# Two extra 512-wide matmuls per item in the last two attentions of a two-model block

## The chip, the cores and the metric

The kernel runs on one core of a Trainium2 chip. The metric is the time of one execution on the device in microseconds (us), as the median of several runs. The clock of TensorE (PE in the rows) is granted by a throttle at one of two levels; a row shows it as a share, where 1.00 is 2.4 GHz and 0.50 is 1.2 GHz.

## What is computed

Two small transformer stacks run one after the other over 256 tokens of width 1024, in fp32 accuracy. The first has a convolution and pooling mixer, a sparse latent attention with a gated recurrence ("dsa" in the kernel), two cross attentions ("x0", "x1") and two expert layers over all 16384 experts. The second, with which the change deals, has two layers:

```python
h = h + even_mixer(rmsnorm(h))   # layer 0: latent causal attention (8 heads) and dilated attention (8 heads)
h = h + swiglu(rmsnorm(h))
h = h + odd_mixer(rmsnorm(h))    # layer 1: sliding window attention with sinks, 16 query heads, 2 kv heads
h = h + swiglu(rmsnorm(h))
```

Each head of these attentions is softmax(q k^T * scale + bias) v, causal over 256 keys. A latent head has 96 dimensions for q and k and 64 for v; all others have 64 and 64. The outputs of all 16 heads go through a 1024 x 1024 projection (e_out, then o_out).

## The kernel before

All engines run one program each, written out by hand, and meet at semaphores. Weights come as a stream of blocks of 128 x 1024; ACT splits each into a high part wH (L483) and DVE or POOL into a low part wL (L493), and both lie in four buffers. A linear layer does three one-pass matmuls for each product (L699 high by high, L700 low by high, L701 high by low), so that the sum is as good as fp32. The attentions use plain fp32 operands instead, which take several passes.

TensorE's results go to 8 banks of PSUM in a fixed order of "groups". bank(key) takes the next group, and reused(n) waits until the group that held the same bank before has been read. w(key) waits on w_low for the block's low part.

attention(kind, ...) runs all attentions. An item is a head and a query tile tt of 128 tokens; with tt = 0 it sees 128 keys, with tt = 1 it sees 256. "mla" (layer 0: heads 0 to 7 latent, 8 to 15 dilated) and "swa" (layer 1) have 16 heads, so 32 items, and the loop has 32 + 5 = 37 turns. In turn i TensorE does the scores S of item i (L756), the transposes PT of the probabilities of item i - 2 (L765), and the product O with the values of item i - 5 (L774). DVE adds the bias (L1542), takes the maximum (L1553) and scales the output (L1559, L1561); ACT takes the exponential (L1184) and copies the transposed probabilities back (L1193). After the loop 16 transposes (L783) turn the outputs, ACT and DVE split them (L1133, L1498), and the projection begins. At the start of the loop TensorE does S of items 0, 1 and 2 and then waits for the probabilities of item 0.

The score matmuls have the head's dimensions as their rows: 96 in the latent heads, 64 in the others. Before an attention all weight blocks that fit into the four buffers are split; in the attention no block is consumed.

Of the kernel before, what the change touches and what calls it, by code (L numbers as in the profile page):

```python
# [18 lines left out]
P = 128  # L19
# [7 lines left out]
NBUF = 4  # L27
# [46 lines left out]
def attention_items(kind):  # L74

    heads = {"x0": 4, "x1": 4, "dsa": 8, "mla": 16, "swa": 16}[kind]
    return [(h, tt) for h in range(heads) for tt in range(NT)]
# [3 lines left out]
DEEP = 4  # L81
AHEAD = 40
POOLED = AHEAD + 3


CKV, IK, IQ, HQ, HF, HG = 8, 9, range(10, 14), range(14, 18), range(18, 22), range(22, 26)
# [197 lines left out]
def build_stacks(nc, x, mem, vecs, cst, w_stream, iw_w, sinks, rel_bias, c_cnt, c_neg, c_masks, c_bucket,  # L284
# [15 lines left out]
    bank_of, before, holder, turn = [], [], {}, 0  # L300
# [9 lines left out]
    with ExitStack() as ctx:  # L310
        def sb(name, shape, dt=F32):
            return ctx.enter_context(nc.sbuf_tensor(name, shape, dt))

        def sem(name):
            return ctx.enter_context(nc.semaphore(name))

        def stage(*wanted):

            with ExitStack() as scope:
                held = [scope.enter_context(nc.sbuf_tensor(name, [P] + list(shape), dt)) for name, shape, dt in wanted]  # L320
                return [t[tuple([slice(None)] * (len(w[1]) + 1))] for t, w in zip(held, wanted)]
# [8 lines left out]
        _, memH, memL = stage(("mem_before", [MEM0], F32), ("memH", [DC, T], F32R), ("memL", [DC, T], F32R))  # L330
        _, att_L, att_P, att_PT, att_O, att_OTH, att_OTL = stage(
            ("att_before", [ATT0], F32), ("att_L", [DEEP, 258], F32), ("att_P", [DEEP, 258], F32),
            ("att_PT", [DEEP, 256], F32), ("att_O", [2, 1024], F32), ("att_OTH", [8, 256], F32R),
            ("att_OTL", [8, 256], F32R))
# [9 lines left out]
        _, rel_bucket, rel_rows = stage(("rel_before", [MEM0 - 1024], F32), ("rel_bucket", [512], F32),  # L344
                                        ("rel_rows", [512], F32))
# [47 lines left out]
        wH, wL = sb("wH", [P, NBUF, BLK], F32R), sb("wL", [P, NBUF, BLK], F32R)  # L393
# [11 lines left out]
        psum = [ctx.enter_context(nc.psum_tensor(f"bank{i}", [P, 512], F32)) for i in range(ALL_BANKS)]  # L405
# [27 lines left out]
        w_high, w_low = sem("w_high"), sem("w_low")  # L433
# [51 lines left out]

        pools = [range(BNO[(f"peer{l}q", 8, 0)], BNO[(f"peer{l}u", 0)] + POOLED) for l in range(2)]

        def split_low(eng, b, i=0):

            if isinstance(i, int) and any(b in (r.start, r.stop) for r in pools):  # L490
                eng.wait_ge(w_low, b)
            eng.wait_ge(w_high, i * 4 + (b + 1))
            eng.tensor_tensor(wL[:, b % NBUF, :], raw(b), wH[:, b % NBUF, :].bitcast(F32),  # L493
                              ALU.subtract).then_inc(w_low, 1)
# [6 lines left out]
        def feed(eng, n):  # L501

            if id(eng) not in fed:
                return
            nxt, split, own = fed[id(eng)]
            while nxt < len(blocks) and (nxt < NBUF or last_read(nxt - NBUF) < n):
                if own(nxt):
                    split(eng, nxt)
                nxt += 1
            fed[id(eng)][0] = nxt  # L510

        def read_of(eng, key):

            n = NO[key]
            feed(eng, n)
            eng.wait_ge(read_by[reader[n]], rank[n])
# [13 lines left out]
        def att_span(kind, tt):  # L530

            return T if kind in ("x0", "x1") else (tt + 1) * P
# [17 lines left out]
        def probs_done(eng, kind, j):  # L550

            if kind in ("x0", "x1"):
                read_of(eng, (kind, "S", j))
            else:
                feed(eng, NO[(kind, "S", j)])
                eng.wait_ge(att_probs, probs_base[kind] + j + 1)
# [114 lines left out]
        def _(pe):  # L671
            at = [0]
            stands = [0]

            def bank(key):

                n = NO[key]
                assert n == at[0], (key, n, at[0])
                at[0] += 1
                reused(n)  # L680
                return psum[bank_of[n]]

            def reused(n):

                if before[n] is not None:
                    pe.wait_ge(read_by[reader[before[n]]], rank[before[n]])
# [47 lines left out]
            def token_major(keys, wkeys, src, cols=512, first=0):  # L734

                for tt, key in enumerate(keys, first):
# [5 lines left out]
                                       k == 0, k == DC - 1)  # L742
                    last.then_inc(group_done, 1)

            def attention(kind, q_of, k_of, v_of):
                items = attention_items(kind)
                base = att_base[kind]
                hv = ATT_V[kind]
                for i in range(len(items) + ATT_LAG_O):
                    if i < len(items):  # L750
                        hd, tt = items[i]
                        span = att_span(kind, tt)
                        ps = bank((kind, "S", i))
                        qs, ks = q_of(hd), k_of(hd)
                        for c in range(len(qs)):
                            last = pe.matmul(ps[:, 0:span], qs[c][:, tt * P:(tt + 1) * P], ks[c][:, 0:span],  # L756
                                             start=(c == 0), stop=(c == len(qs) - 1))
                        last.then_inc(group_done, 1)
                    j = i - ATT_LAG_PT
                    if 0 <= j < len(items):  # L760
                        hd, tt = items[j]
                        ps = bank((kind, "PT", j))
                        probs_done(pe, kind, j)
                        for s in range(att_span(kind, tt) // P):
                            last = pe.transpose(ps[:, s * P:(s + 1) * P], att_P[:, j % DEEP, s * P:(s + 1) * P], ident)  # L765
                        last.then_inc(group_done, 1)
                    j = i - ATT_LAG_O
                    if 0 <= j < len(items):
                        hd, tt = items[j]
                        ps = bank((kind, "O", j))  # L770
                        read_of(pe, (kind, "PT", j))
                        ns = att_span(kind, tt) // P
                        for s in range(ns):
                            last = pe.matmul(ps[:, 0:hv], att_PT[:, j % DEEP, s * P:(s + 1) * P], v_of(hd, s),  # L774
                                             start=(s == 0), stop=(s == ns - 1))
                        last.then_inc(group_done, 1)
                read_of(pe, (kind, "O", len(items) - 1))
                for tt in range(NT):
                    for half in range(2):
                        ps = bank((kind, "OT", tt, half))  # L780
                        for c in range(4):
                            cc = half * 4 + c
                            last = pe.transpose(ps[:, c * P:(c + 1) * P], att_O[:, tt, cc * P:(cc + 1) * P], ident)  # L783
                        last.then_inc(group_done, 1)
# [197 lines left out]
            for tt in range(NT):  # L982
                ps = bank(("iw", tt))
                for k in range(DC):
                    for part in hn:
                        last = pe.matmul(ps[:, 0:8], part[:, k, tt * P:(tt + 1) * P].bitcast(F32), iww[:, k, :],
                                         start=(k == 0 and part is hn[0]), stop=(k == DC - 1 and part is hn[1]))
# [14 lines left out]
            for hd in range(4):  # L1002
                last = pe.matmul(ps[:, hd * P:(hd + 1) * P], kl[:, hd * P:(hd + 1) * P], ql[:, hd * P:(hd + 1) * P],
                                 start=True, stop=True)
# [9 lines left out]
            for hd in range(4):  # L1014
# [5 lines left out]
                          stop=True).then_inc(group_done, 1)  # L1020
# [447 lines left out]
        def _(dve):  # L1468
# [100 lines left out]
            def peer(l):  # L1569
# [67 lines left out]
                def rows(i, j):  # L1637
                    if not isinstance(i, int) or j >= 2:

                        dve.wait_ge(g_done, i * 4 + (l * T // 4 + j - 1))  # L1640
                    for m in range(4):
                        k = (4 * j + m) % 8
                        tok = i * 16 + (4 * j + m)
                        dve.tensor_scalar(onehot[:, k, :], iota, slotT[:, 2, bass.ds(tok, 1)], None, ALU.is_equal)  # L1644
                        last = dve.tensor_scalar(onehot[:, 8 + k, :], iota, slotT[:, 1, bass.ds(tok, 1)],  # L1645
                                                 slotT[:, 0, bass.ds(tok, 1)], ALU.is_equal, ALU.mult)
                    last.then_inc(onehots, 1)
# [13 lines left out]
                for j in range(4):  # L1661
                    rows(0, j)
                    split_low(dve, b0 + POOLED + j)
                with dve.Fori(1, T // 16) as i:
                    for j in range(4):
                        rows(i, j)
                        split_low(dve, b0 + POOLED + j, i)
                with dve.Fori(0, (N_KEYS - AHEAD - T // 4) // 4) as i:
                    for j in range(4):
                        split_low(dve, b0 + POOLED + T // 4 + j, i)  # L1670
                dve.wait_ge(g_read, (l + 1) * T // 4)
# [457 lines left out]
```

## Time and profile before

| | us |
|---|---|
| median of 3 runs | 3132.38 |
| lowest, highest | 3124.88, 3133.9 |
| profiled execution | 3136.3 |
| its span | 3134.5 |
| PE busy | 2918.3 (93%) |
| DVE busy | 1978.9 (63%) |
| ACT busy | 1466.4 (47%) |
| mean granted clock of PE | 0.94 |

By line, the chain that ended last is PE at L699 22%, L700 21%, L701 21%, then the splits of weights (POOL 4%, DVE 3%, ACT 3%) and, of the attentions, L756 2% and L774 2%, L765 1%. The profile is one execution. PE's busy time counts an instruction from its start to its modelled end; neighbouring matmuls overlap, so distances between starts tell their pace better than their durations. The granted clock is a record of its own and is shown for any stretch of time.

### The profile page before, as it was taken

To read this page: it belongs to the slowest core of one execution; us is meant where nothing else is said; L and a number is where in the kernel's file an instruction comes from. 1 tells how busy PE (TensorE), PEld (TensorE's weight loads), DVE (VectorE), ACT (ScalarE), POOL (GpSimd) and SP (SyncE) were. 2 spreads that over 40 slices of the span, in tenths; PEclk is the share of its full clock that TensorE was granted. 3 is DMA by queue.
4 is the path that set the end of the run, shared out by engine and by line. 5 is a ranking of instruction groups with operands and counts; after the bars stand their busy time and mean duration, and the time that the engine had idled before them with its cause. 6 is when DMAs were issued, how large, how long until landed. Compare 5 with 4: busy or idle time off the path is not lost.

```text
span 3134.5 us, 57237 instructions
## 1 busy us (share of the span) xinstructions
PE 2918.3 (93%) x19610; PEld 2711.0 (86%) x19610; DVE 1978.9 (63%) x4205; ACT 1466.4 (47%) x2397; POOL 338.8 (11%) x167
## 2 busy tenths in 40 slices
PE   7889799999999998968999999999997899999998
PEld 6889699999988887858998999988886779987998
DVE  6545942886577676685597887466775655445554
ACT  5444344444455555444444444455554444443443
POOL 0003685000000000000277000000000000000000
PEclk9998899999999999889899999999998879995999
DMA  4434366445666663322456445676664315450444
GB/s 155 153 148 148 134 211 199 172 171 188 230 250 239 241 242 132 121 78 98 149 178 210 174 170 186 217 254 238 245 236 149 120 54 177 176 220 6 162 182 155
DMA packets 140448, 546.16 MB, mean 174 GB/s; under 512 B 15784, under 2 KB 81592, under 8 KB 83616
## 3 DMA queue, kind: packets, MB, share of 16 engines
q1 hardware_dynamic: 63216, 455.38, 40.1%
q10 hardware_dynamic: 73728, 67.14, 6.9%
q0 software_dynamic: 3376, 21.88, 1.8%
q8 instruction: 86, 1.41, 0.2%
q14 instruction: 42, 0.34, 0.0%
HBM read 505.53 MB, written 40.91 MB: 174 GB/s over the span
## 4 chain that ended last, share of the span: by engine, by line
PE 74%; DVE 9%; DMA 6%; ACT 5%; POOL 4%; issue 2%; SPq 0%; ACTq 0%; DVEq 0%
PE bank L699 22%; PE bank L700 21%; PE bank L701 21%; POOL wL L493 4%; PE bank L855 4%; ACT wH L483 3%; DVE wL L493 3%; DMA ring<-in_w_stream 3%; DMA act_parked<-act_out 2%; PE bank L756 2%; PE bank L774 2%; PE bank L765 1%; PE bank L712 1%; DVE act_out L1486 1%; DVE h L1518 1%
## 5 line engine op out<-in xcount | busy, mean ns | idle before, releaser
L493 DVE TENSOR_TENSOR wL<-ring,wH 128x1024 fp32r<-128x1024 f32 x744 | 906.9, 1225 | 750.9 <-ACT wH L483 750.3
L699 PE MATMUL bank<-hnH,wH 128*128 128x256 f32 x3648 | 1066.9, 292 | 61.2 <-DVE hnL L1492 44.1
L700 PE MATMUL bank<-hnL,wH 128*128 128x256 f32 x3648 | 1045.4, 287 | 0.0
L701 PE MATMUL bank<-hnH,wL 128*128 128x256 f32 x3648 | 1044.7, 286 | 0.0
L483 ACT ACTIVATE wH<-ring 128x1024 fp32r<-128x1024 f32 x864 | 906.3, 1055 | 274.0 <-DMA ring<-in_w_stream 128.6
L699 PEld LDWEIGHTS bank<-hnH,wH 128*128 128x128 f32 x3648 | 711.6, 195 | 71.8 <-issue 57.7
L700 PEld LDWEIGHTS bank<-hnL,wH 128*128 128x128 f32 x3648 | 714.5, 196 | 0.1
L701 PEld LDWEIGHTS bank<-hnH,wL 128*128 128x128 f32 x3648 | 712.8, 195 | 0.0
L699 PE MATMUL bank<-wH,wgtH 128*128 128x512 f32 x1024 | 400.1, 391 | 4.5 <-issue 4.5
L700 PE MATMUL bank<-wL,wgtH 128*128 128x512 f32 x1024 | 399.5, 390 | 0.0
L701 PE MATMUL bank<-wH,wgtL 128*128 128x512 f32 x1024 | 399.5, 390 | 0.0
L493 POOL TENSOR_TENSOR wL<-ring,wH 128x1024 fp32r<-128x1024 f32 x120 | 314.6, 2641 | 140.6 <-ACT wH L483 140.5
L1244 ACT ACTIVATE act_out<-bank 128x256 f32<-128x256 f32 x256 | 98.1, 383 | 393.5 <-PE bank L701 334.7
L699 PEld LDWEIGHTS bank<-wH,wgtH 128*128 128x128 f32 x1024 | 192.9, 188 | 45.0 <-issue 5.1
L1268 ACT ACTIVATE wgtH<-gates 128x256 fp32r (+1 forms) x256 | 107.2, 419 | 258.0 <-PE bank L701 257.7
L701 PEld LDWEIGHTS bank<-wH,wgtL 128*128 128x128 f32 x1024 | 193.0, 188 | 40.4
L700 PEld LDWEIGHTS bank<-wL,wgtH 128*128 128x128 f32 x1024 | 193.1, 189 | 40.2
L1645 DVE TENSOR_SCALAR onehot<-con,slotT 128x128 f32<-128x128 f32 x512 | 175.2, 342 | 0.0
L1644 DVE TENSOR_SCALAR onehot<-con,slotT 128x128 f32<-128x128 f32 x512 | 144.1, 281 | 18.6 <-ACT slotT L1283 18.6
L855 PE MATMUL bank<-onehot 128*128 128x128 f32 x1024 | 136.3, 276 | 8.8 <-DVE onehot L1645 8.8
L855 PEld LDWEIGHTS bank<-onehot 128*128 128x128 f32 x1024 | 126.5, 193 | 9.2 <-DVE onehot L1645 9.2
L1152 ACT ACTIVATE sq<-h 128x256 f32<-128x256 f32 x96 | 37.0, 415 | 181.1 <-DVE h L1518 172.0
(338 smaller groups left out, 3612.7 us busy)
## 6 DMA issues: line engine op xcount, KB each, us to landing
ring<-in_w_stream SPq DMA_DIRECT2D x432, 1024.0 KB, 4.9
act_parked<-act_out ACTq DMA_DIRECT2D x256, 128.0 KB, 3.6
act_in<-act_parked ACTq DMA_DIRECT2D x256, 128.0 KB, 2.7
sw_bias<-in_c_swa POOLq DMA_DIRECT2D x1, 4096.0 KB, 13.9
relb_rows<-rel_table POOLq DMA_DIRECT2D x1, 2048.0 KB, 9.6
h_parked<-h POOLq DMA_DIRECT2D x2, 1024.0 KB, 6.5
h_back<-h_parked POOLq DMA_DIRECT2D x2, 1024.0 KB, 6.3
od_relb<-relb_rows POOLq DMA_DIRECT2D x2, 1024.0 KB, 8.2
```

What stands on the lines that cost most here:

```text
L483: eng.activation(wH[:, b % NBUF, :], raw(b), ACT.Copy).then_inc(w_high, 1)
L493: eng.tensor_tensor(wL[:, b % NBUF, :], raw(b), wH[:, b % NBUF, :].bitcast(F32), ALU.subtract).then_inc(w_low, 1)
L699: pe.matmul(dst, lh, rh, start=start, stop=False, skip_group_check=True)
L700: pe.matmul(dst, lh, rl, start=False, stop=False, skip_group_check=True)
L701: return pe.matmul(dst, ll, rh, start=False, stop=stop, skip_group_check=True)
L756: last = pe.matmul(ps[:, 0:span], qs[c][:, tt * P:(tt + 1) * P], ks[c][:, 0:span], start=(c == 0), stop=(c == len(qs) - 1))
L774: last = pe.matmul(ps[:, 0:hv], att_PT[:, j % DEEP, s * P:(s + 1) * P], v_of(hd, s), start=(s == 0), stop=(s == ns - 1))
L855: last = pe.matmul(psacc[j][:, m * P:(m + 1) * P], onehot[:, k, :], onehot[:, 8 + k, :], start=True, stop=True)
L1244: act.activation(act_out[:, c % 2, :], psum[c % BANKS][:, 0:T], ACT.Gelu_apprx_tanh).then_inc(u_read, 1)
L1268: act.activation(wgtH[:, c % 2, :].unsqueeze(1), gates[:, bass.ds(i * 4 + c, 1), :], ACT.Copy).then_inc(wgt_high, 1)
L1644: dve.tensor_scalar(onehot[:, k, :], iota, slotT[:, 2, bass.ds(tok, 1)], None, ALU.is_equal)
L1645: last = dve.tensor_scalar(onehot[:, 8 + k, :], iota, slotT[:, 1, bass.ds(tok, 1)], slotT[:, 0, bass.ds(tok, 1)], ALU.is_equal, ALU.mult)
```

## The change

A function spin() is added for TensorE. It runs behind the O product of a turn, in the attentions mla and swa alone, from turn 2 on. It looks up the next group's bank, waits until that bank may be written, waits for the next weight block that is not used yet, and runs SPINS = 2 matmuls with that block's high part as both operands (128 columns of it as the stationary one, 512 as the moving one). The result lands in the next group's bank, whose own first matmul overwrites it (start=True). No semaphore is raised.

```diff
+SPINS = 2
...
+            def spin():
+
+                b, n = stands[0], at[0]
+                reused(n)
+                pe.wait_ge(w_low, b + 1)
+                for _ in range(SPINS):
+                    pe.matmul(psum[bank_of[n]][:, :], wH[:, b % NBUF, 0:P], wH[:, b % NBUF, 0:512], start=True, stop=True)
+
             def attention(kind, q_of, k_of, v_of):
...
                         last.then_inc(group_done, 1)
+                    if kind in ("mla", "swa") and i >= 2:
+                        spin()
                 read_of(pe, (kind, "O", len(items) - 1))
```

## Rows read from the trace of the kernel before

**Rows 1.** The page: granted clock of PE in 40 slices, in tenths.
```profile
PEclk9998899999999999889899999999998879995999
```

**Rows 2.** Table by stretch: start:end, us, busy per engine (instructions), PEclk, DMA share, GB/s.
```profile
core 0: us, PE busy (x) PEld busy (x) DVE busy (x) ACT busy (x) POOL busy (x), PEclk, DMA share, GB/s
...
2490.00:2507.00 17.00, 17.00 (x70) 15.22 (x70) 11.25 (x43) 8.14 (x32) 0.00 (x0) 0.50 0.01 1
2508.00:2536.00 28.00, 28.00 (x93) 20.20 (x93) 14.93 (x57) 10.93 (x45) 0.00 (x0) 0.50 0.00 1
...
2542.00:2546.40 4.40, 3.68 (x16) 3.28 (x16) 2.15 (x4) 2.12 (x4) 0.00 (x0) 0.50 0.00 0
2546.40:2550.00 3.60, 2.48 (x21) 2.49 (x22) 0.90 (x2) 0.27 (x1) 0.00 (x0) 1.00 0.00 0
2827.00:2879.00 52.00, 52.00 (x171) 37.36 (x170) 29.64 (x132) 20.74 (x82) 0.00 (x0) 0.50 0.00 1
...
2890.80:2894.60 3.80, 3.76 (x17) 3.76 (x18) 0.00 (x0) 0.00 (x0) 0.00 (x0) 0.50 0.01 4
```

**Rows 3.** Chain that ended last in mla: start, us, engine and line.
```profile
2508.11 1.15 PE bank L756 x2
...
2535.87 1.15 PE bank L756 x2
```

**Rows 4.** The same chain in swa: one pair, and the last pair's start.
```profile
2831.50 1.15 PE bank L756 x2
2832.65 0.62 PE bank L765 x2
2833.27 0.32 PE bank L774 x2
2833.59 0.72 PE bank L756 x2
2834.32 0.40 PE bank L765
2834.72 0.75 PE bank L774 x4
...
2879.13 1.15 PE bank L756 x2
```

**Rows 5.** Table by stretch around TensorE's gap, mla and swa.
```profile
2484.98:2488.40 3.42, 1.43 (x9) 1.09 (x10) 3.14 (x9) 2.35 (x8) 0.00 (x0) 1.00 0.73 287
...
2819.50:2822.90 3.40, 2.04 (x15) 1.65 (x13) 1.21 (x2) 2.45 (x3) 0.00 (x0) 1.00 0.70 280
```

**Rows 6.** Table by stretch in the dsa attention.
```profile
1368.00:1372.00 4.00, 4.00 (x17) 3.35 (x17) 3.64 (x13) 2.37 (x9) 0.00 (x0) 0.50 0.01 4
...
1376.00:1384.00 8.00, 5.63 (x35) 4.19 (x36) 7.43 (x27) 3.94 (x16) 0.00 (x0) 1.00 0.00 0
```

**Rows 7.** Timeline of two 512-wide matmuls at the low clock.
```profile
2480.88 0.63 PE L699 MATMUL bank<-wH,ml_nH 128*128 128x512 f32 x1
...
2481.31 0.52 PE L700 MATMUL bank<-wL,ml_nH 128*128 128x512 f32 x1
```

**Rows 8.** Table by stretch in the outs loop of an expert layer.
```profile
900.00:1100.00 200.00, 200.00 (x884) 165.62 (x883) 140.17 (x221) 108.55 (x147) 0.00 (x0) 1.00 0.68 242
```

**Rows 9.** Chain that ended last: the last weight split before swa.
```profile
2821.69 1.23 DVE wL L493
```

**Rows 10.** Timeline: output transposes and the product behind them, dsa and mla.
```profile
1389.32 1.97 PE L783 MATMUL bank<-con,att_O 128*128 128x128 f32 x16 [0.77 <-DVE att_O L1561]
...
1393.60 0.39 PE L699 MATMUL bank<-att_OTH,wH 128*128 128x256 f32 x1 [2.32 <-DVE att_OTL L1498]
...
2542.36 3.68 PE L783 MATMUL bank<-con,att_O 128*128 128x128 f32 x16 [0.45 <-DVE att_O L1561]
...
2547.52 0.39 PE L699 MATMUL bank<-att_OTH,wH 128*128 128x256 f32 x1 [1.48 <-DVE att_OTL L1498]
```

## The prediction

> **What bounds the kernel now.** I read the page's clock line first [rows 1]: it is 9 over most of the span, with 7 in the 33rd slice and 5 in the 37th. The question is what lies in those two and what TensorE does there. The table by stretch answers it [rows 2]. In the first half of the "mla" attention (heads of 96 rows) TensorE is busy 17.00 of 17.00 us at a granted clock of 0.50, in its second half (64 rows) 28.00 of 28.00 at 0.50, in "swa" 52.00 of 52.00 at 0.50. 0.50 is the lower level, 1.2 GHz. DVE is busy 14.93 of 28 and 29.64 of 52 us, ACT less. So both attentions are bound by TensorE's own stream at half clock, over 97 us of these three rows alone, and no wait sets their pace.
>
> The chain of waits shows it at a finer grain. Two items (one head, both query tiles) are a repeating pair. In the 64-row heads the big score product starts at 2508.11 and for the seventh time after it at 2535.87 [rows 3], so a pair takes 27.76 / 7 = 3.97 us. In swa [rows 4] it is again 3.97: 1.15 + 0.62 + 0.32 + 0.72 + 0.40 + 0.75 = 3.96, with no piece of another engine, and 2831.50 to 2879.13 are 12 pairs. A 96-row pair is 13 matmul records, and 70 of them stand in 17.00 us: 3.2 us.
>
> Why the clock is down: before each attention TensorE runs dry until the first softmax is out. Around that gap it was busy 1.43 of 3.42 us (mla) and 2.04 of 3.40 (swa), still at 1.00 [rows 5], and right behind these stretches the clock is 0.50, to the end of the attention. The "dsa" attention tells what can bring it back [rows 6]: after its gap it too ran at 0.50, busy 4.00 of 4.00 us to 1372 with matmuls of all 128 rows, and by 1376 the clock had risen; it stayed at 1.00 though TensorE was then busy only 5.63 of 8.00. So a full-height stream raised it; the mix of 96 or 64 rows with 64-column outputs did not, in 28 and 52 us without a pause; and a far thinner mix keeps it once it is up.
>
> **The change part by part.** It removes and moves nothing. It adds, from i = 2 to 36 of the 37 turns of each of the two loops, two matmuls: 35 x 2 = 70 per attention, 140 in all, 128 rows by 512 columns in the one-pass type.
>
> *Price of one.* At the low clock the nearest rows are two 512-wide products of the va group, whose starts lie 2481.31 - 2480.88 = 0.43 us apart [rows 7]; 70 are 30.1 us. At the full clock the outs loop of the expert stage has 884 of them in 200.00 us, 0.226 each [rows 8]; 70 are 15.8 us. Their weight loads are inside both numbers.
>
> *The waits it adds.* reused(n) waits for the reader of the bank which the next group would wait for anyway. w_low waits for the first block of the output projection; it is split in order, and the last split before swa starts at 2821.69 [rows 9], before the first turn that spins, and none is made in the attention. I take 0 for both; if a reader were late, everything queued on TensorE would stand behind it, but the next group would have stood there too. No DMA is added, and SP, POOL, ACT and DVE get no instruction.
>
> *mla, if the clock comes back.* At full clock a 96-row pair's own work is 3.2 / 2 = 1.6 us, with four added matmuls 1.6 + 0.9 = 2.5: a gain of 0.7. A 64-row pair is 3.97 / 2 + 0.90 = 2.89: a gain of 1.08. DVE needs about 14.93 / 28 x 3.97 = 2.1 us for a pair, so it is not yet the bound. From 2488.4, where the clock fell, to 2508.1 are 6.2 pairs of the first kind: -4.3 us. Then 7 of the second: -7.6. The last turns, 6.5 us from 2535.87 to the transposes at 2542.36, become 3.25 + 6 x 0.45 = 5.95: -0.5. The transposes of the output: in dsa at 1.00 from their start to the next product 1393.60 - 1389.32 = 4.28 us, in mla at 0.50 it is 2547.52 - 2542.36 = 5.16 [rows 10]: -0.9. Two turns that ran at 1.00 before 2488.4 get 0.9 dearer. Sum -12.4. I take off 2.9 for hand-overs at the tighter pace (about 0.1 a pair, 1.3) and for one turn or two of a first stretch at low clock (1.6), and say -9.5, with -13 to -5 as its range.
>
> Will it come back here? The mix with the added work lies between the 96-row mix that stayed at 0.50 and the 128-row mix that rose. About a third of its time (1.7 of 4.9 us in a pair at low clock) is now the full-height stream, and the rest is three quarters high. That is near to dsa's, so I say yes, and soon. The 64-row half then inherits the full clock, and dsa shows that keeping it takes little.
>
> *swa, if the clock stays down.* It has no 96-row half: it starts cold, since the first added matmul comes behind the first transpose, that is behind the same gap. Its own pair is 3.97 us with half-height score products, the added 1.7 us of full height make 30% of 5.7 us. That is further from dsa's mix than mla's is, and its neighbour in the trace is the 64-row mix at 0.50. I take low clock to the end: 70 x 0.43 = 30.1 us, all on the path, since the chain is TensorE throughout. A weight load that the long matmul now hides can give back some: a 64-row big product takes 1.15 in the chain, and 0.2 of that over 16 pairs is 3 us. Bounds 25 to 31, taken 29.
>
> *Sum.* -9.5 + 29 = +19.5 us. The profiled execution took 3136.3 us (span 3134.5); that gives 3155.8. The median of the runs shown is 3132.4, 3.9 lower; on it the forecast is 3152.
>
> **What the Trainium skill says to this.** The row first: from 2542.00 to 2546.40 TensorE ran 16 transposes and nothing else, at 0.50, and behind them the clock is 1.00 [rows 2]. "TensorE: Matmul & The Clock Gate", Part 4, says that work in transpose mode does not count as activity for the clock in the same way. By that rule the transposes in the loop would weaken the mix, and the third rival below would gain; the trace disagrees, and I keep that rival small. The same page, Part 1, has it that activity releases the throttle; taken as busy time it would give these stretches the full clock already, and the added matmuls would cost 140 x 0.226 = 32 us and buy nothing. The rows at 28.00 of 28.00 and 0.50 speak against that reading.
>
> **The rivals.**
> (a) *Both attentions come back to the full clock* (the other side). Mechanism: the full-height share is enough for the 64-row mix too, or swa's clock doesn't fall at all because the added matmuls fill waits behind the gap. For it: dsa rose within a few us of such a stretch; swa offers over 52 us in which a denser moment could do. Against: 52.00 us at 0.50 without the clock ever rising. Price: 12 pairs in [rows 4] and 2 before them, 14 x -1.08 = -15.1; one pair at the low clock first +2.8; last turns -0.5; transposes -0.9; the output projection, which now spends its first 3.8 us at 0.50 [rows 2], -1.9; hand-overs +1.4: -14.2. With mla's -9.5 that is -23.7: 3109 us. The point from which it decides: each cold swa pair costs 4 x 0.43 = 1.72, each warm one gives 1.08; with mla's 9.5 and the 3 of the ends the whole comes out at zero if the clock rises at about the tenth of 14 pairs, and faster if earlier.
> (b) *Neither comes back* (the added matmuls are load and nothing else). For it: both stages sat at 0.50 though TensorE was never idle. Against: dsa. Price: 29 in each, +58: 3190 us.
> (c) *swa rises late*, somewhere past the middle, or mla late: within 9 us of before, or in between.
>
> **How the numbers follow.** Forecast 0.56; (a) 0.28; (b) 0.07; (c) 0.09, of which 0.06 lies within 0.3%, 0.02 faster, 0.01 slower. The bound of 0.3%, 9.4 us, is about what a measurement of this kernel can tell from no change. So faster 0.30, same 0.06, slower 0.64. The forecast's own range is its parts' bounds, 25 - 13 to 31 - 5: +12 to +26, or 3144 to 3158, and some more for the scatter of the medians (3124.9 to 3133.9 before): to 3163. As (a) holds 0.28, the range for 8 in 10 goes down to it: 3104 to 3163.
>
> **What would show it.** The clock by stretch: 1.00 in mla from a few us behind its first transposes on, 0.50 in swa. Pairs of 2.5 to 2.6 us and 2.9 to 3.0 in mla, 5.5 to 5.7 in swa. The added matmuls 0.23 apart in mla, 0.43 in swa. The clock rising only after the start of the output projection behind swa. The forecast is wrong if swa's row shows 1.00 (then the mix of row heights was no bar), or if mla's shows 0.50; and its sizes are wrong if DVE's share goes to 0.9 at full clock, as then the added matmuls are hidden under DVE.

## The result, and the profile after

The changed kernel takes 3149.12 us (median of 7 runs, 3143.15 to 3160.76) against 3133.9 (7 runs, 3124.88 to 3139.85): ratio 1.0053, 95% interval 1.0034 to 1.0073. The medians lie 15 us apart, and the ratio makes it some 17. The forecast was 3152 on a median of 3132.4. The profiled execution took 3143.15 us, its span is 3141.4.

The table by stretch of the kernel after (start:end, us, busy time by engine, granted clock, DMA) answers to [rows 2] and [rows 5]. The first five rows are mla, the last three swa.

```profile
core 0: us, PE busy (x) PEld busy (x) DVE busy (x) ACT busy (x) POOL busy (x), PEclk, DMA share, GB/s
2471.80:2475.20 3.40, 1.99 (x6) 1.55 (x7) 1.94 (x7) 1.92 (x8) 0.00 (x0) 0.50 0.71 289
2475.20:2478.60 3.40, 3.40 (x12) 2.92 (x11) 1.42 (x4) 1.52 (x6) 0.00 (x0) 0.50 0.00 0
2478.60:2492.00 13.40, 13.40 (x90) 11.92 (x90) 10.25 (x41) 7.63 (x30) 0.00 (x0) 1.00 0.01 2
2493.00:2518.00 25.00, 25.00 (x132) 15.96 (x131) 16.08 (x62) 12.05 (x48) 0.00 (x0) 1.00 0.00 1
2523.40:2527.20 3.80, 1.87 (x16) 1.63 (x16) 2.48 (x4) 2.06 (x4) 0.00 (x0) 1.00 0.00 0
...
2810.00:2886.00 76.00, 76.00 (x221) 48.23 (x221) 29.12 (x130) 20.15 (x81) 0.00 (x0) 0.50 0.00 1
2886.00:2891.60 5.60, 5.60 (x18) 3.70 (x18) 1.88 (x9) 1.26 (x5) 0.00 (x0) 0.50 0.00 0
2891.60:2895.20 3.60, 3.60 (x24) 2.98 (x23) 1.35 (x7) 0.38 (x1) 0.00 (x0) 0.99 0.02 7
```

TensorE is busy all the time in both, as before. What differs is the clock: in mla it is 0.50 for 6.8 us from the gap on and then 1.00 to the end, where it was 0.50 from 2488.4 on to the end of the attention; in swa it is 0.50 for the 76 and 5.6 us of two rows, and comes back in the last turns only, where no score products are left.

The stages can be measured from the first score product to the first product of the projection. The timeline of the kernel before has for the start of mla and the end of TensorE's idle time behind it (2.21 us), and for the start and end of swa (the end of mla is in [rows 10]):

```profile
2483.46 1.14 PE L756 MATMUL bank<-ml_k,ml_q 96*128 96x128 f32 x6 [0.71 <-ACT ml_vA L1160]
...
2486.81 0.30 PE L765 MATMUL bank<-con,att_P 128*128 128x128 f32 x1 [2.21 <-ACT att_P L1184]
...
2820.77 1.14 PE L756 MATMUL bank<-sw_k,sw_q 64*128 64x128 f32 x6 [0.37 <-ACT sw_v L1160]
...
2890.84 0.58 PE L699 MATMUL bank<-att_OTH,wH 128*128 128x256 f32 x1 [1.48 <-DVE att_OTL L1498]
```

and the kernel after, mla and swa:

```profile
2469.75 1.14 PE L765 MATMUL bank<-ml_k,ml_q 96*128 96x128 f32 x6 [0.99 <-ACT ml_vA L1171]
...
2527.24 0.39 PE L700 MATMUL bank<-att_OTH,wH 128*128 128x256 f32 x1 [1.97 <-DVE att_OTL L1509]
...
2800.85 1.14 PE L765 MATMUL bank<-sw_k,sw_q 64*128 64x128 f32 x6 [0.36 <-ACT sw_v L1171]
...
2899.02 0.39 PE L700 MATMUL bank<-att_OTH,wH 128*128 128x256 f32 x1 [1.97 <-DVE att_OTL L1509]
```

(The lines have moved: scores L765, transposes L774, outputs L783, output transposes L794, the added matmuls L752.) mla: 64.06 us before, 57.49 after, -6.6. swa: 70.07 before, 98.17 after, +28.1. Together +21.5. The spans differ by 6.9 only, because this execution reached mla 13.7 us earlier, through code that was not changed. The experiments below show that as scatter: with the front part always the same, mla begins between 2474 and 2485 us in them, while a stage repeats within 0.1 us as long as the clock moves at the same places. So stages are compared below, and medians beside them.

One such place differs in mla itself. In the kernel before the clock fell at about 2488.3, which is 4.9 us after the first score product; in the kernel after it fell at 2471.8, 2.1 us after it. An unchanged mla in which it also fell 2.1 us after the start took 64.78 us (the run with the matmuls in swa alone, below). Against that one the change gives mla -7.3 us; 0.7 of it is missing from the -6.6 because the kernel before had the full clock a little longer.

The chain of waits after (start, us, engine and line) has one pair of items in the 64-row half of mla, then one in swa, and around it the big score products of swa's items 5 and 31:

```profile
2494.33 0.62 PE bank L765 x2
2494.95 0.37 PE bank L774 x2
2495.32 0.17 PE bank L783 x2
2495.49 0.52 PE bank L752 x2
2496.01 0.41 PE bank L765 x2
2496.43 0.26 PE bank L774
2496.69 0.39 PE bank L783 x4
2497.08 0.52 PE bank L752 x2
...
2810.20 1.15 PE bank L765 x2
...
2827.88 1.15 PE bank L765 x2
2829.03 0.62 PE bank L774 x2
2829.65 0.32 PE bank L783 x2
2829.97 0.96 PE bank L752 x2
2830.93 0.72 PE bank L765 x2
2831.65 0.41 PE bank L774
2832.05 0.75 PE bank L783 x4
2832.81 0.96 PE bank L752 x2
...
2886.75 1.15 PE bank L765 x2
```

The own work of the swa pair is 3.97 us, the same pieces as in [rows 4]; two pairs of added matmuls of 0.96 make it 5.89. In mla the same kind of pair takes 3.26 us (the sum of its pieces; 3.27 by the starts): own work 2.22, added 1.04.

### The profile page after: what moved, and what is told of

Its sections match the earlier page's. It is cut to its first block, busy times and chain, and to the rows that moved or that the text cites. A ratio compares the mean times of both kernels' runs of the same rounds, so it can differ in the third digit from the quotient of the medians.

```text
span 3141.4 us, 57587 instructions
## 1 busy us (share of the span) xinstructions
PE 2921.8 (93%) x19750; PEld 2699.1 (86%) x19750; DVE 1976.4 (63%) x4205; ACT 1464.1 (47%) x2397; POOL 338.6 (11%) x167
## 4 chain that ended last, share of the span: by engine, by line
PE 73%; DVE 9%; DMA 6%; ACT 5%; POOL 4%; issue 2%; SPq 0%; ACTq 0%; DVEq 0%
PE bank L700 21%; PE bank L702 20%; PE bank L701 20%; POOL wL L494 4%; DMA ring<-in_w_stream 4%; PE bank L866 4%; ACT wH L484 3%; DVE wL L494 3%; DMA act_parked<-act_out 2%; PE bank L752 2%; PE bank L765 2%; PE bank L783 1%; PE bank L774 1%; PE bank L713 1%; DVE act_out L1497 1%
```

## Experiments

**One attention at a time.** Which of the two carries which sign.

```diff
-                    if kind in ("mla", "swa") and i >= 2:
+                    if kind == "mla" and i >= 2:
```

> The added matmuls stand in mla alone, swa is as before. My theory (the full-height work brings the clock back in mla, not in swa): the mla stage, from its first score product to the first product of the projection, is about 57.5 us as in the changed kernel (64.1 before), clock 1.00 in it but for its first 7 us or so; swa 70 us as before. Time 6.6 us under the kernel before, 3127, ratio 0.998. Rival (the two attentions work on each other, or the scatter of the rest of the kernel hides it): mla over 62 us, ratio 1.000 or more.

Measured: 3125.94 us, ratio 0.9977 (0.9966 to 0.9988), 7 us under before. mla 57.52 us, swa 70.08. Both are the stages expected, each to 0.1 us: what is added in mla does not act on swa.

```diff
-                    if kind in ("mla", "swa") and i >= 2:
+                    if kind == "swa" and i >= 2:
```

> The added matmuls stand in swa alone. My theory: clock 0.50 in swa to the end of the loop, pairs of 5.9 us, the swa stage 98 us against 70 before, time +28 us, 3162, ratio 1.009; mla 64 us at 0.50. Rival (swa's clock stayed down by accident of that one execution): the clock is 1.00 in most of swa, the stage is under 70 us and the time at or under the kernel before.

Measured: 3154.63 us (4 runs), ratio 1.0076 (1.0051 to 1.0102), 7 us less than expected. swa 98.18 us with some 88.7 of them at 0.50, mla 64.78. That swa stays at the low clock is no accident of one execution. The table by stretch of both versions, each in its mla and then its swa; the first two rows are the version with the matmuls in mla alone:

```profile
2491.40:2539.80 48.40, 46.46 (x273) 34.49 (x271) 32.65 (x122) 23.35 (x87) 0.00 (x0) 1.00 0.00 1
2822.00:2883.00 61.00, 59.51 (x205) 44.40 (x205) 34.09 (x147) 23.69 (x87) 0.00 (x0) 0.50 0.00 1
...
2480.20:2538.00 57.80, 57.31 (x212) 45.91 (x210) 32.94 (x124) 24.45 (x93) 0.00 (x0) 0.50 0.00 1
2815.00:2903.00 88.00, 86.98 (x250) 54.85 (x251) 34.15 (x152) 24.26 (x95) 0.00 (x0) 0.50 0.00 1
```

**Half the rows.** The forecast rested on the height of the rows: mla's 96 against swa's 64. This tests it inside mla, by the added matmuls themselves. They write one bank further on; a control writes that same bank with 128 rows.

```diff
-                b, n = stands[0], at[0]
+                b, n = stands[0], at[0] + 1
...
-                    pe.matmul(psum[bank_of[n]][:, :], wH[:, b % NBUF, 0:P], wH[:, b % NBUF, 0:512], start=True, stop=True)
+                    pe.matmul(psum[bank_of[n]][:, :], wH[0:64, b % NBUF, 0:P], wH[0:64, b % NBUF, 0:512], start=True, stop=True)
...
-                    if kind in ("mla", "swa") and i >= 2:
+                    if kind == "mla" and i >= 2:
```

> As mla alone, but the added matmuls use 64 rows of the tile instead of 128 and write the bank after the next one. Same count, same columns, same busy time. If the height of the rows counts for the clock: it stays 0.50 in mla, the stage is 64 + 70 x 0.48 = about 97 us. If busy time or columns alone count: it rises as with 128 rows, stage about 57 us.

> The control for the version with 64 rows: mla alone, two matmuls of 128 rows and 512 columns per turn, written to the bank after the next one. If rows were what counted: as with the next bank, mla stage about 57.5 us, clock 1.00 but for its first us. If the other bank was what kept the clock down: 0.50 and about 98 us as with 64 rows.

Measured with 64 rows: 3173.17 us (2 runs), ratio 1.013 (1.0096 to 1.0164), mla 98.32 us. With 128 rows: 3128.16, ratio 0.9986 (0.9967 to 1.0004), mla 57.52. The table by stretch has the whole of mla with 64 rows in its first row, then mla with 128 rows from the rise of the clock on:

```profile
2483.10:2579.40 96.30, 93.31 (x288) 63.68 (x288) 36.87 (x133) 27.30 (x101) 0.00 (x0) 0.50 0.03 10
...
2490.50:2539.00 48.50, 46.56 (x273) 34.59 (x271) 32.68 (x122) 23.43 (x87) 0.00 (x0) 1.00 0.00 1
```

Same count, same columns, TensorE busy 93.31 of 96.30 us, and the clock never comes back. Halving the rows turned a gain of 7 us into a loss of 34 in the stage. So being busy, with the same matmuls and columns per turn, did not raise the clock here; what made the difference was the height of the added matmuls, by itself or by what it brings with it.

It brings a second change with it, in the pace. The chain of waits has the same first turns in the kernel after (two rows) and with 64 rows (the next two), from the first added pair to the fourth score product; the last two rows are two pairs of items further on, with 64 rows:

```profile
2473.65 0.87 PE bank L752 x2
...
2478.15 0.74 PE bank L765 x2
...
2485.07 1.15 PE bank L752 x2
...
2491.03 1.15 PE bank L765 x2
...
2526.21 0.85 PE bank L765 x2
...
2536.29 0.85 PE bank L765 x2
```

Both at 0.50, the same work took 4.50 us with 128 rows and 5.96 with 64, so it came a quarter less densely. In the 64-row half of mla it came faster: 10.08 us for two pairs is 5.04 a pair, less than the 5.89 of swa. Whether the height alone held the clock down, or partly the slower pace, is not separated.

**Four instead of two in swa.**

```diff
-                        spin()
+                        spin(SPINS if kind == "mla" else 2 * SPINS)
```

> Two added matmuls per turn in mla, four in swa. If swa stayed cold because the full-height share of its mix was too small, four bring the clock to 1.00: a pair is then 1.99 + 8 x 0.26 = 4.1 us, the swa stage about 72 to 76 us, less than with two (98), time about 3132 + 4 - 7 = 3130. If something else holds the clock down in swa, a pair is 3.97 + 8 x 0.48 = 7.8 us, the stage about 130 us, time about 3185.

Measured: 3138.15 us (10 runs, 3129.93 to 3150.81), ratio 1.0016 (1.0000 to 1.0033). Right in direction: the clock does come back in swa. But it does so late, in the profiled execution after 37.5 us, as the table by stretch has it:

```profile
2807.40:2844.90 37.50, 35.82 (x95) 23.06 (x95) 11.88 (x51) 9.19 (x35) 0.00 (x0) 0.50 0.00 0
2844.90:2888.00 43.10, 43.10 (x220) 29.68 (x220) 22.94 (x103) 15.49 (x61) 0.00 (x0) 1.00 0.00 1
```

The stage takes 91.37 us, not 72 to 76. While the clock is low a turn is dearer than ever. Why it rose at that turn and not before is not shown, nor whether it rises at the same turn in the other executions; the times of the 10 runs scatter by 21 us, which a changing turn would explain but does not prove.

**Hold instead of raise.** If the gap in front of the first probabilities drops the clock, and holding it takes less than raising it, matmuls belong into the gap, where TensorE has nothing else to do. On the kernel before:

```diff
+            def fill(ps, count):
+                b = stands[0]
+                pe.wait_ge(w_low, b + 1)
+                for _ in range(count):
+                    pe.matmul(ps[:, :], wH[:, b % NBUF, 0:P], wH[:, b % NBUF, 0:512], start=True, stop=True)
...
                         ps = bank((kind, "PT", j))
+                        if kind in ("mla", "swa") and j == 0:
+                            fill(ps, 10)
                         probs_done(pe, kind, j)
```

> No matmul is added per turn. Instead ten 512-wide ones stand before TensorE's wait for the first probabilities of mla and of swa, in the 2.2 us in which it is idle. Theory (the gap is what drops the clock, and holding it takes far less than raising it, as dsa showed): 1.00 through both attentions; a pair is then bound by DVE at about 2.3 us or by TensorE's 2.2, stages about 45 us each (64 and 70 before), time about 3090, ratio 0.986. Rival (the attentions' own thin mix cannot hold the clock): it falls to 0.50 within some turns, stages 60 to 70 us, time within 0.3% of before.

Measured: 3084.89 us (4 runs), ratio 0.985 (0.9807 to 0.9892), 49 us under before and 64 under the changed kernel (by the medians). mla 41.57 us, swa 45.85. The chain of waits in mla has the ten matmuls (L750) at the place of the gap; a pair in swa is at full clock without any added one; and the table by stretch shows the clock:

```profile
2484.67 1.14 PE bank L763 x6
2485.82 2.28 PE bank L750 x10
```

```profile
2815.10 0.63 PE bank L763 x2
...
2817.33 0.63 PE bank L763 x2
```

```profile
2504.00:2519.00 15.00, 15.00 (x89) 10.95 (x89) 13.72 (x55) 10.46 (x42) 0.00 (x0) 1.00 0.00 1
...
2804.00:2834.40 30.40, 30.33 (x174) 21.81 (x172) 27.56 (x132) 21.08 (x83) 0.00 (x0) 1.00 0.01 2
2834.40:2837.80 3.40, 2.72 (x18) 2.00 (x16) 3.13 (x16) 2.16 (x9) 0.00 (x0) 1.00 0.00 0
2837.80:2841.20 3.40, 3.11 (x14) 2.96 (x14) 1.30 (x9) 0.80 (x3) 0.00 (x0) 0.50 0.01 2
```

A pair takes 2.23 us, DVE is busy 27.56 of 30.40 us and is nearly the bound now. The thin 64-row mix holds the full clock for more than 30 us; it drops only in the last turns, where small pauses come in, for some 7 us. "TensorE: Matmul & The Clock Gate" of the Trainium skill, section "Why this matters for your kernels", advises against idle gaps between bursts of matmuls. Here the trace agrees, and goes further: the idle time before the first transpose is 2.2 us, shorter than the gaps of that table's row, and the two stages are 22 and 24 us shorter with it filled.

**One per turn besides.** The same with one matmul at the end of each turn from 2 on.

```diff
+                    if kind in ("mla", "swa") and i >= 2:
+                        reused(at[0])
+                        fill(psum[bank_of[at[0]]], 1)
```

> The ten matmuls in the gap, and one per turn from turn 2 on. Theory: clock 1.00 throughout; a 64-row pair is 2.22 of own work + 2 x 0.26 = 2.74, so the stages are about 48 and 51 us, time about 3100, some 10 above the version with the gap alone if that one holds its clock, and below it if it does not.

Measured: 3098.95 us, ratio 0.9899 (0.9866 to 0.9932); 1.00 in both attentions, stages 47.61 and 51.73 us. The holding matmul is not needed and costs its 6 us in each.

**The change as it is, with the gap filled.**

```diff
                         ps = bank((kind, "PT", j))
+                        if kind in ("mla", "swa") and j == 0:
+                            pe.wait_ge(w_low, stands[0] + 1)
+                            for _ in range(10):
+                                pe.matmul(ps[:, :], wH[:, stands[0] % NBUF, 0:P], wH[:, stands[0] % NBUF, 0:512],
+                                          start=True, stop=True)
                         probs_done(pe, kind, j)
```

> The change as it is, two per turn, with the ten matmuls in the gap before it. Theory (in swa the two per turn could not raise the clock but can hold it): clock 1.00 in both attentions, swa pairs of 3.27 us as the 64-row pairs of mla had in the changed kernel, swa stage about 59 us against 98 with the change alone, mla about 54; time about 3113. Rival (the 64-row mix falls back even so): swa stage over 90 us, 3145.

Measured: 3117.24 us (2 runs), ratio 0.9949 (0.9929 to 0.9969). mla 54.75, swa 59.33 us. The table by stretch for swa:

```profile
2811.60:2870.90 59.30, 57.36 (x304) 38.34 (x304) 39.48 (x165) 28.81 (x102) 0.00 (x0) 1.00 0.02 9
```

The same two matmuls per turn that could not raise the clock in swa in 88 us keep it there, once it has not been lost. This is the plainest pair of the study: swa takes 98.17 us without and 59.33 with ten more matmuls in an idle place.

**The same at nine norms.** Behind a norm's sum TensorE waits some 5 us for the normalised rows. On the version with the gap matmuls:

```diff
+                if name in ("peer0", "mix1", "x1", "peer1", "final", "mix2", "ffn0", "mix3", "ffn1"):
+                    reused(at[0])
+                    fill(psum[bank_of[at[0]]], 20)
```

> As the version with the gap matmuls alone, and in nine norms twenty 512-wide matmuls (4.5 us) behind the norm's sum, where TensorE waits some 5 us for the normalised rows. Theory (each such gap costs a stretch of 6.8 us at 0.50 behind it, worth 3.4 us): up to 9 x 3.4 = 30 us less than the gap version, 3060, ratio 0.976. Rival (the next weights bound the start of those stages, so that a higher clock there buys nothing): no gain, 3085, or a loss of up to 9 us where the matmuls outlast the gap.

Measured: 3080.3 us (4 runs, 3061.76 to 3081.53), ratio 0.9811 (0.9778 to 0.9844). The medians put that 5 us under the gap version, the ratios 12, and the intervals of the two overlap; the time at the low clock fell from about 243 to 170 us of the span. So some 70 us at the low clock went, for 5 to 12 us of time instead of the 30 expected. The rival (the next weights bound those stages) fits that better, but it was not tested; which norms pay was not separated.

## Why the prediction was right, point by point

- *Bound.* Both attentions were TensorE's stream at 0.50. Holding the clock at 1.00 took mla from 64 to 42 and swa from 70 to 46 us, with ten matmuls in each gap as the only other difference.
- *mla comes back, soon.* Right: 0.50 for 6.8 us behind the gap, then 1.00. *swa stays down.* Right, and in two kernels. The reason given, the height of the rows, was argued in the prediction. In mla the 64-row run supports it, with the pace as an open rival. For swa the four-matmul run shows only that more added work can bring the clock back; that its 64-row score products are the reason is not shown.
- *mla's size* was forecast at -9.5, measured -6.6, inside its -13 to -5. The 64-row pair was put at 2.89 us and took 3.27 (seven of them 2494.33 to 2517.24): -4.9 instead of -7.6. Two terms were too small. Own work at the full clock is 2.22 us, not half of 3.97: the big score product goes from 1.15 to 0.62 and the double transpose from 0.62 to 0.37, so some time does not scale with the clock. And an added matmul costs 0.26, not the 0.226 of [rows 8]. The first half, forecast at some -2 with its low stretch, came out even: up to the first 64-row pair 24.6 us in both kernels, since 6.8 us ran with dearer turns at the low clock, and the kernel before had kept the full clock 2.8 us longer. The last turns gave -0.4 and the output transposes, until the projection begins, -1.2 (5.16 to 3.94) instead of -0.9.
- *swa's size* was +29, measured +28.1, by luck: three errors met. An added matmul costs 0.48 there, not the 0.43 of [rows 7], so 70 would have been +33. The 3 us that hidden weight loads were to give back did not come: the big score product takes 1.15 us with the added work too. And swa did not stay at 0.50 to the end: from 2891.6 the last turns and the transposes ran at 1.00, which gave back some 5 us. In numbers: from 2810.20 to 2886.75 are 13 pairs of 5.89 us, 13 x 1.92 = +25.0. The turns ahead of them gave +2.6, the last turns +1.8 (12 added matmuls, 5.8 at 0.48 each), the transposes -1.2. Behind the stage the projection began at full clock, and the rest of the kernel is 1.3 us shorter than before.
- *The signs* came out in part. The 96-row pairs take 2.6 us as said. The 64-row pairs of mla (3.27, not 2.9 to 3.0), those of swa (5.89, not 5.5 to 5.7) and the spacing of the added matmuls (0.26 and 0.48, not 0.23 and 0.43) did not. The clock rose before the projection and not behind its start.
- *The total* of the stages is +21.5, forecast +19.5; the medians moved by 15 only. The difference lies in the parts outside the attentions, which scatter.
- *The waits* of spin() showed nowhere: no idle time stands before L752 in the trace.
- *Rivals.* That both come back is refuted for this kernel; its price (3109) was about what it takes when the clock is kept, 3117 with the gap filled. That neither comes back is refuted in mla. The prediction sees a rule on transposes refuted by the rise at 2546.4 behind mla's transposes and ties it to the third rival; a weaker mix would favour the second as well. The rows are mixed. At the end of swa in the kernel after, 16 transposes run at 1.00. But in swa of the kernel before, 16 transposes ran at 0.50 from 2885.68 on and the clock rose only at about 2894.5, when the projection had run for 3.7 us. So one rise behind transposes does not settle what they count for.
- *What the prediction did not see* is the best use of its own reading. It said that a far thinner mix keeps the clock, and took the gap as given.

## What to carry to other kernels

Where TensorE is busy without a pause and the granted clock still says 0.50, look for the gap in front of that stretch before adding load to it: ten matmuls in each of two idle stretches of some 2.3 us were worth 49 us, two per turn behind them cost 15 to 17. To bring the clock back, added matmuls of 128 rows worked in mla and those of 64 rows did not; and in swa a mix that could not raise the clock in 88 us could hold it. Price added matmuls by the distance of starts in the mix where they will stand, not in a loop of their own kind.

## What the runs showed of the hardware beyond that

- In the same stage 70 matmuls of 128 rows and 512 columns gave the full clock, 70 of 64 rows did not (57.52 and 98.32 us), at a pace that was also slower at first (5.96 against 4.50 us for the same turns).
- A 512-wide matmul between short fp32 ones costs 0.48 us at the low clock and 0.26 at the full one, against 0.43 and 0.226 in a row of its kind: about 0.03 to 0.05 more. What stands in front goes with it: the first three added pairs of swa, behind transposes, take 0.89, 0.85 and 0.86 us in the chain, those behind an output product of 64 columns 0.96. That a weight load has too little to hide behind there is argued, not shown.
- The stages repeat within 0.1 us from kernel to kernel (mla 57.49, 57.52, 57.52, 57.60; swa 98.17, 98.18; unchanged swa 69.99 to 70.08), while whole executions scatter by 15 us. The exception is mla at the low clock, 64.06 and 64.78 us, where the clock fell 4.9 and 2.1 us after the stage's start.
- In the 64-row half of mla, added matmuls of 64 rows and score products of the same height start side by side (2530.24 and 2530.25 us), and the pair takes 5.04 us; with added matmuls of 128 rows the same kind of pair takes 5.89 at the same clock in swa.
